# Two up projections that multiply X scaled by feature only, with the token's norm factor applied to the result in PSUM

## What is computed

```python
h = rmsnorm(x, ffn_pre_g) * (1.0 + sc2) + sh2
u = causal_dwconv(h @ w_up, ffn_conv_w, ffn_conv_b)
u_gate, u_val = jnp.split(u, 2, axis=-1)
f = (jax.nn.silu(u_gate) * u_val) @ w_down
x = x + gt2 * rmsnorm(f, ffn_post_g)
```

## Time and profile before

| | |
|---|---|
| median of three runs | 1058.37 us (1056.8 to 1060.44) |
| span of the profiled execution | 1056.5 us |
| TensorE busy | 1025.1 us, 97% |
| GpSimd, ScalarE, VectorE busy | 689.8, 634.4 and 556.2 us |
| mean granted TensorE clock | 0.997 |

### The profile page before, as it was taken

The page is one execution under the profiler, slowest core; times in us unless marked ns, Lnnn a source line. Parts: engine busy times, 40 slices in busy tenths (PEclk is TensorE's granted clock), DMA queues, the critical chain, the costliest instruction groups (busy, mean ns, idle before and its releaser), DMA issues.

```text
span 1056.5 us, 23232 instructions
## 1 busy us (share of the span) xinstructions
PE 1025.1 (97%) x8537; PEld 966.4 (91%) x8537; DVE 556.2 (53%) x1165; ACT 634.4 (60%) x1133; POOL 689.8 (65%) x306
## 2 busy tenths in 40 slices
PE   7999999999999989999999899999989999999998
PEld 5999999988799979999999799998667699999998
DVE  2577625579874435565522542296566735444400
ACT  4555764477774576666645656744566557666642
POOL 2598899811269855988799287790031075988795
PEclk9999999999999999999999999999999999999999
DMA  9988888655547863777687289865201043665563
GB/s 380 383 306 282 273 307 298 235 191 187 174 146 259 282 236 105 273 235 248 204 279 268 80 283 360 330 239 191 99 21 60 1 140 122 217 193 189 168 217 111
DMA packets 62616, 226.43 MB, mean 214 GB/s; under 512 B 6960, under 2 KB 8272, under 8 KB 61264
## 3 DMA queue, kind: packets, MB, share of 16 engines
q1 hardware_dynamic: 61344, 221.23, 60.5%
q10 hardware_dynamic: 1200, 4.23, 1.4%
HBM read 224.35 MB, written 1.08 MB: 213 GB/s over the span
## 4 chain that ended last, share of the span: by engine, by line
PE 75%; issue 9%; POOL 9%; DVE 3%; ACT 3%; DMA 1%; POOLq 0%; ACTq 0%; DVEq 0%; SPq 0%
PE psL L553 68%; POOL WL L505 8%; PE psO L553 3%; PE psS L553 2%; PE psL L1092 1%; DMA ring<-wts 1%; ACT psL L1685 0%; ACT WH L1155 0%; ACT R L1273 0%; PE psS L1036 0%; ACT L1146 0%; DVE sm L2288 0%; PE psS L1063 0%; PE psS L966 0%; DVE CT L2052 0%
## 5 line engine op out<-in xcount | busy, mean ns | idle before, releaser
L505 POOL TENSOR_TENSOR WL<-ring,WH 128x1024 fp32r<-128x1024 f32 (+1 forms) x282 | 670.4, 2399 | 239.8 <-ACT WH L1155 186.7
L553 PE MATMUL psL<-HR,WH 128*128 128x256 f32 (+1 forms) x3096 | 513.5, 278 | 1.8 <-DVE HR L1796 0.9
L553 PEld LDWEIGHTS psL<-HR,WH 128*128 128x128 f32 (+1 forms) x3096 | 452.6, 187 | 7.5 <-issue 4.8
L553 PE MATMUL psL<-HR,WL 128*128 128x256 f32 x1536 | 396.2, 276 | 0.0
L1155 ACT ACTIVATE WH<-ring 128x1024 fp32r<-128x1024 f32 (+1 forms) x210 | 216.5, 1042 | 107.8 <-PE psL L553 71.9
L553 PEld LDWEIGHTS psL<-HR,WL 128*128 128x128 f32 x1536 | 275.2, 188 | 0.0
L553 PE MATMUL psL<-RR,WH 128*128 128x256 f32 x1356 | 205.2, 277 | 2.4 <-DVE RR L1981 1.2
L553 PEld LDWEIGHTS psL<-RR,WH 128*128 128x128 f32 x1356 | 185.5, 187 | 3.8 <-issue 2.8
L553 PE MATMUL psL<-RR,WL 128*128 128x256 f32 x672 | 145.0, 277 | 0.3 <-POOL WL L505 0.3
L2080 DVE SCALAR_TENSOR_TENSOR CT<-psL,par,CT 128x254 f32<-128x254 f32 (+1 forms) x176 | 80.9, 480 | 107.1 <-ACT CT L1463 102.0
L1454 ACT ACTIVATE WH<-ring 128x1024 fp32r<-128x1024 f32 (+1 forms) x88 | 92.9, 1058 | 71.4 <-PE psL L553 68.0
(11 more groups left out here) (274 smaller groups left out, 1122.8 us busy)
## 6 DMA issues: line engine op xcount, KB each, us to landing
ring<-wts SPq DMA_DIRECT2D x285, 512.0 KB, 4.2
adaring<-ada_w SPq DMA_DIRECT2D x80, 512.0 KB, 4.8
R<-ada_w SPq DMA_DIRECT2D x8, 1024.0 KB, 16.2
ring<-wts SPq DMA_DIRECT2D x16, 384.0 KB, 3.8
R<-cum_dram ACTq DMA_DIRECT2D x8, 512.0 KB, 4.1
R<-wts SPq DMA_DIRECT2D x8, 512.0 KB, 6.4
ring<-wts SPq DMA_DIRECT2D x8, 288.0 KB, 2.8
adaring<-wts SPq DMA_DIRECT2D x4, 512.0 KB, 5.2
```

Source lines behind the costliest of these rows:

```text
L505: nc.gpsimd.tensor_tensor(WL[:, k, 0:n], ring[:, k, 0:n], WH[:, k, 0:n].bitcast(F32), SUB).then_inc(lo_done, 1)
L553: return nc.tensor.matmul(out, lhsT, rhs, start=start, stop=stop)
```

## The change

The projection is linear, so the token's factor can be applied behind it: with g the gain per feature, s the shift and r the factor of a token, `W'(g*x*r + s) = r * (W'(g*x)) + W's`. The new operand is G = g*x alone, in a high part GH and a low part GL, each with two more columns ahead of the 256 tokens, and both of these hold -s. So a product has 258 moving columns, and the first two of a bank are -W's for each output feature, twice.

- The results are scaled in PSUM: VectorE multiplies columns 2 to 257 of each bank by r (`scale`). The two first columns are not scaled and take the place of the missing predecessors in the convolution: they hold -W's, so that the bias can put back W's for all taps alike. VectorE makes that bias for each unit from column 0, the negated sum of the taps (`NWS`, by `tap_sums`) and the convolution's bias. The taps now write all 256 columns. ScalarE's copy waits for both (`f_scaled`).
- Before up1: the root of o1 is written to PSUM. VectorE scales and adds in parts (1, 1, 2, 2 and 2 tiles), ScalarE writes GH from X and the gain as soon as a tile is there, VectorE the low part; TensorE does filler (14) after the first root, then the first three units by two tiles of the operand at a time with the products of the statistic between them. The second root is made while the last of these run; VectorE waits for it before the first `scale`.
- Before up2: for each unit of o2 VectorE writes X times gain to PSUM (`gained`), ScalarE copies it to GH, VectorE subtracts to get GL. The filler and the wait for the root go; the statistic's product stands between the fourth and the fifth tile of the first three units.
- In the up stages VectorE's order in a pair is: scale b = 0, the ada step if there is one, the tap of b = 0, scale b = 1, its tap, then as before. For j = 0 both scales come first. ScalarE's two weight copies of the first pair come behind both copies of results; for the others nothing is moved.
- The norm ahead of layer 2's first projection (`tok2`) keeps `make_h` and `make_hh`.

The core of the diff:

```diff
+T2 = T + 2
-        HX = sb("HX", [P, 4096])
+        HX = sb("HX", [P, 4160])
+        GH, GL = region(HR, 0, a=8, b=T2), region(HR, 8 * T2, a=8, b=T2)
+        NWS = CD[:, :, :].rearrange("p a b -> p (a b)")
+        BCOL = csil
+        def gained(m):
+            return psO[:, m % 2, 0:T]
...
-                        last = triple(psL[:, u % 4, 0:T], WH[:, s, b * P:(b + 1) * P], WL[:, s, b * P:(b + 1) * P],
+                        last = triple(psL[:, u % 4, 0:width], WH[:, s, b * P:(b + 1) * P], WL[:, s, b * P:(b + 1) * P],
...
+            def up_tiles(name, base, tiles):
+                u0, q0 = PLAN.at[name][1], PLAN.q(name)
+                for k in tiles:
+                    pe.wait_ge(h_ready, base + k + 1)
+                    for c in range(3):
+                        if k == 0:
+                            bank_wait(u0 + c)
+                            split_wait(q0 + c)
+                        s = (q0 + c) % SLOTS
+                        last = triple(psL[:, (u0 + c) % 4, 0:T2], WH[:, s, k * P:(k + 1) * P], WL[:, s, k * P:(k + 1) * P],
+                                      g_hi(k), g_lo(k), k == 0, k == 7)
+                        if k == 7:
+                            last.then_inc(lin_done, 1)
...
             pe.wait_ge(rs_ready, 6)
-            fill(u0, 5)
-            stat("stat_ffn1", sq_at, 8, base=13)
-            fill(u0, 6)
-            pe.wait_ge(rs_ready, 7)
-            fill(u0, 4)
-            linear8("up1", 0, 44, h_hi, h_lo, from_count(h_ready, 8), 3, 5, True)
+            fill(u0, 14)
+            pe.wait_ge(pad_lo, 1)
+            up_tiles("up1", 8, (0, 1))
+            out = scratch("stat_ffn1")
+            for part in range(3):
+                for k in (2 * part, 2 * part + 1):
+                    stat_block(out, k, 8, sq_at, 13)
+                if part < 2:
+                    up_tiles("up1", 8, (2 * part + 2, 2 * part + 3))
+            for k in (6, 7):
+                stat_block(out, k, 8, sq_at, 13)
+            up_tiles("up1", 8, (6, 7))
+            linear8("up1", 0, 44, g_hi, g_lo, None, 3, 5, True, T2)
...
-            u0 = PLAN.at["up2"][1]
-            fill(u0, 7)
+            pe.wait_ge(pad_lo, 2)
+            up_tiles("up2", 24, range(4))
             stat_of_sums("stat_ffn2", 3)
-            fill(u0, 7)
-            pe.wait_ge(rs_ready, 12)
-            fill(u0, 4)
-            linear8("up2", 0, 44, h_hi, h_lo, from_count(h_ready, 24), 3, 5, True)
+            up_tiles("up2", 24, range(4, 8))
+            linear8("up2", 0, 44, g_hi, g_lo, None, 3, 5, True, T2)
...
+            def up_operand(j):
+                act.wait_ge(x_ready, j + 1)
+                A(GH[:, j, 2:T2], X[:, j, :], ACT.Identity, scale=lead[:, 16 + j:17 + j]).then_inc(hh_ready, 1)
...
+            up_operand(0)
+            up_operand(1)
+            preload()
+            up_squares(0)
+            for j in (2, 4):
+                up_operand(j)
+                up_operand(j + 1)
+                up_squares(j)
+            up_squares(6)
+            up_operand(6)
+            up_operand(7)
             stat_root("stat_ffn1", D, RS[:, 1, :])
...
-                        A(CT[:, 2 * slot + b, :], psL[:, u % 4, 0:T], ACT.Identity,
+                        act.wait_ge(f_scaled, 4 * (base + j) + 2 * b + 2 + it * 4)
+                        A(CT[:, 2 * slot + b, :], psL[:, u % 4, 2:T2], ACT.Identity,
                           scale=par[:, bass.ds(w0 + 2 * 44 + b * KF + j + it, 1)],
-                          bias=par[:, bass.ds(b0 + b * KF + j + it, 1)]).then_inc(f_begun, 1)
-                        if j == 0:
-                            next_high(b)
+                          bias=BCOL[:, 2 * slot + b:2 * slot + b + 1]).then_inc(f_begun, 1)
+                    if j == 0:
+                        next_high(0)
+                        next_high(1)
...
+                    act.wait_ge(t_ready, 16 + m)
+                    A(GH[:, m - 1, 2:T2], gained(m - 1), ACT.Copy).then_inc(hh_ready, 1)
...
+                def scale(j, slot, b, it):
+                    u = u0 + 2 * j + b
+                    bank = psL[:, u % 4, :]
+                    dve.wait_ge(lin_done, u + 1 + it * 2)
+                    V.tensor_scalar(BCOL[:, 2 * slot + b:2 * slot + b + 1], bank[:, 0:1], NWS[:, bass.ds(b * KF + j + it, 1)],
+                                    par[:, bass.ds(b0 + b * KF + j + it, 1)], MUL, ADD).then_inc(f_scaled, 1)
+                    V.tensor_tensor(bank[:, 2:T2], bank[:, 2:T2], rs, MUL).then_inc(f_scaled, 1)
...
-                            dst = CT[:, 2 * slot + b, back:T]
+                            dst = CT[:, 2 * slot + b, :]
-                                dst, psL[:, us[b] % 4, 0:T - back],
+                                dst, psL[:, us[b] % 4, 2 - back:T2 - back],
```

More of the change, by code:

```diff
@@ L580, in triple, with unit @@
                 return mm(out, wl, hi, False, last)
-            def unit(u, q, nchunks, hi, lo, rounds=0, sizes=(8, 8, 6), operand=None):
+            def unit(u, q, nchunks, hi, lo, rounds=0, sizes=(8, 8, 6), operand=None, width=T):
                 bank_wait(u, rounds)
@@ L603, in thin_products, with late_unit @@
                     mm(psL[0:32, u % 4, T:2 * T], weights, rhs, True, True)
-            def late_unit(u, q, nchunks, hi, lo, operand=None, thin=False):
+            def late_unit(u, q, nchunks, hi, lo, operand=None, thin=False, width=T):
                 bank_wait(u)
-                out = psL[:, u % 4, 0:T]
+                out = psL[:, u % 4, 0:width]
                 for c in range(nchunks):
@@ L643, in together, with linear8 @@
                             last.then_inc(lin_done, 1)
-            def linear8(name, first, count, hi, lo, operand=None, joint=0, late=0, thin=False):
+            def linear8(name, first, count, hi, lo, operand=None, joint=0, late=0, thin=False, width=T):
                 q0, u0 = PLAN.q(name) + first, PLAN.at[name][1] + first
-                if joint:
+                if joint and operand:
                     together(u0, q0, joint, hi, lo, operand)
@@ L653, in linear8 @@
                 for c in range(joint, done):
-                    late_unit(u0 + c, q0 + c, 1, hi, lo, thin=thin and c == joint)
+                    late_unit(u0 + c, q0 + c, 1, hi, lo, thin=thin and c == joint, width=width)
                 rounds = (count - done) // SLOTS
@@ L1181, in wide, with shift_pads @@
                 return view.rearrange("p a b -> p (a b)")
+            def shift_pads(shift):
+                A(GH[:, :, 0:2], shift.unsqueeze(2).to_broadcast([P, KD, 2]), ACT.Copy, scale=-1.0).then_inc(pad_hi, 1)
             def make_hh(shift, base):
@@ L1402, in square_place, with scale_and_square @@
                 return psS[:, m % 2, 0:T]
-            def scale_and_square(name, dst, gains, use, before):
+            def scale_and_square(name, dst, gains, use, before, pads=None):
                 u0 = PLAN.at[name][1]
@@ L1417, in scale_and_square @@
                     act.sem_inc(lin_free[u % 4], 1)
+                    if pads is not None and m == 0:
+                        shift_pads(pads)
                     feed(u)
@@ L2061, in _ @@
             dve.wait_ge(evac_done, 8)
-            add_normed(MIX, RS[:, 0, :], 0)
-            dve.wait_ge(x_ready, 8)
-            dve.wait_ge(rs_ready, 7)
-            make_h(mod[:, 24:32], lead[:, 16:24], RS[:, 1, :], 8)
-            def ffn(name, wname, base, between):
-                u0 = PLAN.at[name][1]
-                w0 = PAR[wname][0]
-                def conv(j, slot, it=0, uses=0):
+            root = sbank("stat_o1")[:, 0:T]
+            part = psL[:, (PLAN.at["up1"][1] + 3) % 4, :].rearrange("p (a b) -> p a b", b=T)
```

93 lines of the change are left out of this document (68 added, 25 removed).

## The result

The changed kernel took 1071.85 us (median of 4 runs, 1068.59 to 1072.77), the kernel before 1059.12 (4 runs, 1056.8 to 1060.44): a ratio of 1.0119, interval 1.01 to 1.0138. It is slower by 1.2%, where 0.7% faster was forecast, and far above the range (1048.3 to 1056.0). The profiled execution took 1070.99 us, its span 1069.0, 12.5 more than before.

What follows compares the result with a forecast made beforehand. TensorE, busy 97% of 1056.5 us, was taken as the bound, with idle and filler ahead of up1 and up2. 3.95 + 5.5 - 1.9 - 0.3 = 7.25 us gained: 1051.1 us, range 1048.3 to 1056.

Steps and rivals of the forecast that it cites:

- Parts 1 and 2: Starts of up1 and up2: less idle and filler ahead of them, net gains of 3.95 and 5.5 us.
- an 8.59: Up1's shared block: time in us its 72 products took before, used to forecast the block's end at 401.65.
- The 0.4 for the late weight copy: Start of up1: loss of 0.4 us because ScalarE splits the first pair's next weights only behind both copies.
- Part 4: VectorE inside up1: added scaling just fits TensorE's time for two pairs; 0.3 us charged for jitter.
- the second rival: Up1: VectorE doesn't hold the pace, 0.45 us per two pairs; 2.6 us lost, 1053.7 us; chance 0.17.
- Part 3: Up stages: 2112 products with 258 columns instead of 256, priced in proportion to columns, -1.9 us.
- The term of 1.9 us: Cost of two more columns in the up stages' 2112 products, at 0.9 ns a product.
- The 15-column row: Profile row: a 15-column product costs 0.113 us, like one of 256; taken as a sign of a floor.
- the 32-weight-column row: Profile row: 256-column products with 32-column weights also cost 0.113 us; taken as evidence against free columns.
- Free columns: Rival for the up stages: the two added columns cost nothing; gain 9.15 us, 1049.2 us; chance 0.15.
- The slower rival: Up stages: 258-column products, rows off multiples of 1024 bytes, cost 0.119 us each; 1060.8 us; chance 0.08.
- the bound of 5.5: Up stages: upper end for a wide product's extra cost, 5.5 ns, from up1's shared block; 11.6 us over 2112.

Runs made afterwards that it cites:

- the narrow runs: Changed kernel with the shift's two columns left out of the up1 and up2 products (256 columns), five variants: 1058.54 to 1063.42 us.
- the second profile: The kernel before, unchanged, profiled a second time: 1058.17 us, beside 1061.35.

## Why the prediction was wrong

- **Parts 1 and 2 came out right.** Counted from the end of o1, up1 began after 8.13 us (forecast 8.12) and its block ended after 20.30 (20.42): 4.47 gained for 4.35. Up2's block ended 9.90 us after o2 (9.37): 4.97 for 5.5, short because its own products are 258 wide. Up1's block has them too, but the forecast had priced it by an 8.59 that was slow already (below), which is luck. Operands, low parts and the second root were in time. The 0.4 for the late weight copy isn't seen: TensorE is busy 119.93 of 119.93 us in the stretch behind.
- **Part 4 came out right by luck.** VectorE's longer pairs hid behind TensorE, which never waited in the stretches. But two pairs took VectorE 11.6 us and not the 10.8 worked out: a scaling took 0.60 us and not 0.5, and behind three of four it stood still 0.85 us until ScalarE's copy was done, where 0.6 to 0.7 had been worked in. At the forecast pace TensorE would have needed 96 x 0.1144 = 11.0 us, so VectorE would have fallen behind by some 0.6 us in every two pairs (an estimate), as the second rival had it with 0.45. Only the dearer products hid it, and the narrow runs, with products of 118.5, show it.
- **Part 3 is the step that failed**: "The row with the same operand type and width is the nearest: proportional, 0.113/256 = 0.44 ns a column, 0.9 ns a product". A pace at 256 columns says nothing of the price of the 257th unless it is known to be set by the columns. It wasn't: 248 columns cost the same 113.2. The term of 1.9 us was 7.7 + 7.6 in the long stretches (7.8 ns a product and not 0.9), and the mechanism behind it was wrong and not only its size. The 15-column row was read rightly as a floor of 113; the wrong turn was to take the 32-weight-column row as proof against any floor. It speaks only against the weight load as the floor's cause, for both rows show the same 113.
- The rule of the Trainium skill ("TensorE: Matmul & The Clock Gate", LDWEIGHTS) weighed there would have made the columns free. A floor is there, at 248 and 256 columns; that the weight load sets it isn't shown, and the row of 32 weight columns stands against it. Free columns beyond 256 are ruled out by 258.
- **The slower rival named the place and was given 0.08.** It had "the product of 258 columns, whose operand rows no longer start at multiples of 1024 bytes" at 5.5 ns. Both halves exist and each is enough: columns 8.2 ns, rows 5 ns. Its price was too low by 2.3 ns a product, and 4.3 was rightly the point from which it decides. It deserved more, because nothing in the trace bounded the price from above; the bound of 5.5 came from a block that had another reason to be slow. That block's 8.59 us is the slow one of two levels, 72 x 117.6 ns = 8.47; in the second profile the same block ran at 113.2.
- **Not in the prediction at all**: untouched products got dearer, 4.7 us in the down stages. Why isn't known.

## What to carry to other kernels

Before a product gets wider, find out whether its pace is set by its columns: run it narrower, and if that saves nothing, it stands on a floor whose edge may be the present width. A rider of two columns on 2,112 products cost more than two whole heads were worth. Keep the moving operand's rows at the places where they are known to run fast: a shift of 32 bytes, which a field added ahead of a buffer can bring, cost 28 us here. And read the pace as window over count; TensorE's busy share, its waits and its clock were all perfect in the slower kernel. And a path that stays hidden behind a slower one hasn't been confirmed: VectorE's 0.8 us too many per two pairs showed only when the products got quicker.

## What the runs showed of the hardware that wasn't expected

- fp32r products with 128 weight columns, back to back, at the full clock: 113.2 ns at 248 and 256 moving columns, 121.5 at 258, 123.2 at 272.
- 256 columns from rows begun 32 bytes further on: 118.1 to 118.3 ns; from rows 1,032 bytes apart: 118.5 to 120.3; from rows as they were: 113.2. From rows 1,056 bytes apart: 118.2. The trace doesn't show addresses, and no simple rule was found: a boundary of 64 bytes that each product pays for by itself would give 115.7 for the 1,056.
- Equal products have two paces, 113.2 and 117.6 ns, which last for whole blocks or stages, and the same program took one or the other in the same block of two executions.
- VectorE operations with two SBUF inputs of 256 columns: 0.47 us long beside an idle GpSimd, and 2.1 to 2.6 us each while GpSimd made a low part.
